# Turning the recurrence's input with a transposing DMA in two f16 halves instead of two TensorE transposes

## What is computed

```
h = rmsnorm(x, norm_g);  proj = h @ w_in            # 4096 x 3072
sb_q, sb_k, sb_v, sb_gate, lru_x, lru_gate, xa_q, xa_gate = split(proj)
sb_out  = stick_breaking_attention(rmsnorm(q), rmsnorm(k), v)     # 8 heads x 64
xc      = causal_depthwise_conv(lru_x, conv_w, conv_b)            # width 4, 256 channels
r, i    = sigmoid(xc @ w_rg + b_rg), sigmoid(xc @ w_ig + b_ig)    # 4 blocks of 64
log_a   = -8 * r * softplus(-lambda)
h_t     = exp(log_a) * h_(t-1) + sqrt(1 - exp(2 log_a)) * (i * xc)   # over time
xa_out  = memory_cross_attention(xa_q, mem)                       # 4 heads, 256 tokens
y       = concat(sb_out * silu(sb_gate), h * silu(lru_gate), xa_out * silu(xa_gate))
out     = x + y @ w_out
```

## Time and profile before

| what | value |
|---|---|
| median of 3 runs | 1570.18 us (1567.96 to 1570.65) |
| the profiled execution | 1568.22 us |
| its span in the trace | 1566.5 us, mean granted TensorE clock 0.994 |
| PE busy | 1514.1 us, 97% of the span |
| DVE busy | 1029.6 us, 66% |
| ACT busy | 882.3 us, 56% |
| POOL busy | 314.7 us, 20% |
| DMA queue q1 (SP's) | 201 MB, 52.8% of 16 engines' time |

### The profile page before, as it was taken

How to read it: one execution, slowest core, us unless ns; L and a number is a source line. 1 busy time by engine, 2 the same in 40 slices (tenths; PEclk the granted TensorE clock), 3 DMA queues, 4 the chain that set the end, 5 groups by cost and what they waited for, 6 DMA issues and landing times.

```text
span 1566.5 us, 29731 instructions
## 1 busy us (share of the span) xinstructions
PE 1514.1 (97%) x10828; PEld 741.4 (47%) x10828; DVE 1029.6 (66%) x1874; ACT 882.3 (56%) x1593; POOL 314.7 (20%) x305
## 2 busy tenths in 40 slices
PE   4899899999999999999999999999999999999996
PEld 1344444444444444444444444444444444444452
DVE  5889566766666666656676666666665667666674
ACT  5887455654455664455565446566445556544661
POOL 2122112222122222111222211222211222221120
PEclk9999999999999999999999999999999999999999
DMA  9355555456455445554545545544556454555545
GB/s 367 136 168 105 132 112 118 111 125 141 117 125 123 104 118 133 125 136 105 123 104 130 141 117 119 129 102 117 136 119 142 104 117 111 127 142 120 120 90 136
DMA packets 425928, 201.63 MB, mean 129 GB/s; under 512 B 394592, under 2 KB 395040, under 8 KB 424736
## 3 DMA queue, kind: packets, MB, share of 16 engines
q1 hardware_dynamic: 425600, 200.98, 52.8%
q10 hardware_dynamic: 288, 0.13, 0.0%
HBM read 55.53 MB, written 50.53 MB: 68 GB/s over the span
## 4 chain that ended last, share of the span: by engine, by line
PE 87%; ACT 4%; DVE 4%; SPq 2%; issue 2%; DMA 1%; POOL 0%; ACTq 0%; DVEq 0%; POOLq 0%
PE bank L1792 26%; PE bank L1793 26%; PE bank L1794 26%; PE bank L1871 2%; SPq L492 2%; PE bank L1986 2%; PE bank L1836 2%; PE bank L1857 1%; PE bank L1880 1%; ACT w_pair L867 1%; PE bank L1926 0%; PE bank L1921 0%; PE bank L1823 0%; PE bank L1923 0%; PE bank L1922 0%
## 5 line engine op out<-in xcount | busy, mean ns | idle before, releaser
L1792 PE MATMUL bank<-w_pair,x_hi 128*128 128x512 f16 x1536 | 585.0, 381 | 13.8 <-DVE w_pair L1231 4.8
L1793 PE MATMUL bank<-w_pair,x_hi 128*128 128x512 f16 x1536 | 584.1, 380 | 0.0
L1794 PE MATMUL bank<-w_pair,x_lo 128*128 128x512 f16 x1536 | 584.0, 380 | 0.0
L1124 ACT ACTIVATE spare<-xy,columns 128x1024 f16<-128x1024 f32 x32 | 36.7, 1148 | 399.6 <-DVE columns L1650 399.6
L1792 PEld LDWEIGHTS bank<-w_pair,x_hi 128*128 128x128 f16 x1536 | 150.7, 98 | 190.1 <-issue 13.9
L1794 PEld LDWEIGHTS bank<-w_pair,x_lo 128*128 128x128 f16 x1536 | 150.7, 98 | 182.6 <-issue 2.4
L1793 PEld LDWEIGHTS bank<-w_pair,x_hi 128*128 128x128 f16 x1536 | 150.8, 98 | 166.4 <-issue 2.5
L1792 PE MATMUL bank<-wo_pair,y_hi 128*128 128x512 f16 x480 | 181.9, 379 | 1.2 <-issue 1.2
L1793 PE MATMUL bank<-wo_pair,y_hi 128*128 128x512 f16 x480 | 181.9, 379 | 0.0
L1794 PE MATMUL bank<-wo_pair,y_lo 128*128 128x512 f16 x480 | 181.9, 379 | 0.0
L736 POOL TENSOR_TENSOR fail_and_take<-fail_and_take,seen 128x512 f32<-128x512 f32 x32 | 42.5, 1327 | 684.2 <-ACT fail_and_take L888 684.2
(11 more groups left out here) (267 smaller groups left out, 2397.8 us busy)
## 6 DMA issues: line engine op xcount, KB each, us to landing
xy<-in_x SPq DMA_DIRECT2D x32, 512.0 KB, 3.6
spare<-in_x SPq DMA_DIRECT2D x31, 512.0 KB, 4.2
out<-spare SPq DMA_DIRECT2D x30, 512.0 KB, 2.7
gate_kept<-gate SPq DMA_DIRECT2D x32, 256.0 KB, 2.3
v_kept<-v_sb SPq DMA_DIRECT2D x32, 256.0 KB, 2.1
fail_and_take<-v_sb SPq DMA_DIRECT2D x64, 128.0 KB, 2.3
q_kept<-q_t SPq DMA_DIRECT2D x32, 256.0 KB, 4.0
k_kept<-k_t SPq DMA_DIRECT2D x32, 256.0 KB, 4.5
```

The lines of the kernel that those rows point to most:

```text
L1124: act.activation(y_halves[:, 0, :], xy[:, :], ACT.Copy, scale=y_top[:, :]).then_inc(s["y_high"], 1)
L1792: pe.matmul(dst, hi[:, k, :], pair[:, 0, k, :], start=k == 0, stop=False)
L1793: pe.matmul(dst, hi[:, k, :], pair[:, 1, k, :], start=False, stop=False)
L1794: last = pe.matmul(dst, lo[:, k, :], pair[:, 0, k, :], start=False, stop=k == KD - 1)
```

## The change

lru_x leaves PSUM as two f16 halves (`lx_halves`): ACT writes the high one in place of the f32 copy, scaled by a power of two (VDOWN); DVE makes the low one in a new instruction in `silu_lru`, 128 x 256 from PSUM, ahead of the instruction that was there. A new transposing DMA of both halves at once (128 x 512 f16) into `lx_turned` is issued by SP ahead of `q_t`'s high half, behind a wait for `gate_l` of the same tile (in step 31: ahead of the low halves). The two transposes on PE go, with their waits. DVE's `convolution` waits for that DMA and adds the two halves into `conv_in` instead of copying from PSUM. The scale that ACT applied is multiplied into the taps once, in step 0. `gate_products` takes over the wait for `y_mixed` that stood ahead of the transposes.

```
--- before.py
+++ after.py
@@ -123,7 +123,7 @@
         q_raw = sb("q_raw", [P, HS, HD])
         k_raw = sb("k_raw", [P, HS, HD])
         xq_raw = sb("xq_raw", [P, HX, HD])
-        lx_raw = sb("lx_raw", [P, LW])
+        lx_halves = sb("lx_halves", [P, 2, LW], F16)
         v_sb = sb("v_sb", [P, 2, 2, GC], F16)
         k_t = sb("k_t", [P, 2, 2, HS // 2, HALF + P], F16)
         q_t = sb("q_t", [P, 2, HS // 2, P], F16)
@@ -146,6 +146,7 @@
         y_halves = spare[:, D:2 * D].bitcast(F16).rearrange("p (a c) -> p a c", a=2)
         xq_halves = spare[:, 2 * D:2 * D + LW].bitcast(F16).rearrange("p (a c) -> p a c", a=2)
         rs_diag = spare[:, 2 * D + LW:2 * D + LW + P]
+        lx_turned = spare[:, 2 * D + LW + P:2 * D + 2 * LW + P].bitcast(F16).rearrange("p (a h t) -> p a h t", a=2, t=P)
         x_halves = x_t32[:, :, :].rearrange("p k t -> p (k t)").bitcast(F16).rearrange("p (a c) -> p a c", a=2)
         h_sb = spare[:, KD * GC - D - LW:KD * GC - D].rearrange("p (h t) -> p h t", t=P)
         ident = sb("ident", [P, P])
@@ -157,6 +158,7 @@
         g_in = given[:, 0:KD]
         g_mem = given[:, KD:2 * KD]
         at = 2 * KD + LH * TAPS
+        taps = given[:, 2 * KD:at]
         cw = given[:, 2 * KD:at].rearrange("p (h j) -> p h j", j=TAPS)
         cb, brg, big, lam = [given[:, at + i * LH:at + (i + 1) * LH] for i in range(4)]
         gq, gk, gxq, gxk = [given[:, at + 4 * LH + i:at + 4 * LH + i + 1] for i in range(4)]
@@ -243,7 +245,7 @@
         HEADS = bank[7]
 
 
-        names = """turned_lx lx_evac k_gained qk_high qk_low k_halo out0_read scores sig masked scan w w_high w_low heads
+        names = """lx_evac k_gained qk_high qk_low k_halo out0_read scores sig masked scan w w_high w_low heads
             q_read k_read xa_read lru_read sg_read v_hi v_read q_sum k_sum xq_sum rs_mid rs_done normed
             gate_x gate_l gate_sb xa_scores mx_done neg_done p_done p_high p_low
             conv gates_done gates_read tanh_done beta_steps ui_done beta_done u_done h_done
@@ -258,6 +260,7 @@
         w_turned = sem("w_turned")
         p_turned = sem("p_turned")
         y_turned = sem("y_turned")
+        lx_arrived = sem("lx_arrived")
         late_y_high = sem("late_y_high")
         x_loaded = sem("x_loaded")
         xt_loaded = sem("xt_loaded")
@@ -591,6 +594,12 @@
                     have_dma(sp, kept["q"], n - 1)
                     have(sp, s["xa_scores"], n - 1)
                     for part, signal in ((0, s["qk_high"]), (1, s["qk_low"])):
+                        if part == (1 if last else 0):
+                            have(sp, s["gate_l"], n)
+                            have(sp, s["lx_evac"], n - 1)
+                            if isinstance(n, int) and n == 0:
+                                sp.wait_ge(m_kv, MT)
+                            turn(lx_turned.rearrange("p a h t -> p (a h) t"), lx_halves[:, :, :].rearrange("p a c -> p (a c)"), lx_arrived)
                         have(sp, signal, n)
                         q_half, k_half, xq_half = halves_of_heads(n, part)
                         turn(q_t[:, part], q_half, qk_turned)
@@ -1059,7 +1068,8 @@
                 if A:
                     have(act, proj_done[3], n)
                     u = unscale[:, G_LRU:G_LRU + 1]
-                    act.activation(lx_raw[:, :], PROJ[1][:, 0:LW], ACT.Copy, scale=u)
+                    have_dma(act, lx_arrived, n - 1)
+                    act.activation(lx_halves[:, 0, :], PROJ[1][:, 0:LW], ACT.Copy, scale=VDOWN)
                     act.activation(gate[:, p, D // 2:D // 2 + LW], PROJ[1][:, LW:GC], ACT.Sigmoid, scale=u
                                    ).then_inc(s["lru_read"], 1)
 
@@ -1360,11 +1370,11 @@
 
                 def convolution(d):
 
-                    have(dve, s["turned_lx"], n - d)
+                    have_dma(dve, lx_arrived, n - d)
                     dve.tensor_copy(conv_in[:, :, 0:TAPS - 1], conv_in[:, :, P:P + TAPS - 1]).then_inc(s["halo"], 1)
                     have(dve, s["halo"], n - d)
-                    dve.tensor_copy(conv_in[:, :, TAPS - 1:], SMALL[:, 2 * P:4 * P].rearrange("p (h t) -> p h t", t=P)
-                                    ).then_inc(s["lx_evac"], 1)
+                    dve.tensor_tensor(conv_in[:, :, TAPS - 1:], lx_turned[:, 0, :, :], lx_turned[:, 1, :, :], ALU.add
+                                      ).then_inc(s["lx_evac"], 1)
                     have(dve, s["lx_evac"], n - d)
                     if isinstance(n, int) and n == 1:
                         dve.wait_ge(qk_turned, 96)
@@ -1480,6 +1490,9 @@
                     weights_low(1)
 
                 def silu_lru():
+                    have(dve, s["lru_read"], n)
+                    dve.scalar_tensor_tensor(lx_halves[:, 1, :], PROJ[1][:, 0:LW], VDOWN, lx_halves[:, 0, :],
+                                             ALU.mult, ALU.subtract)
                     silu(s["lru_read"], s["gate_l"], PROJ[1][:, LW:GC], slice(D // 2, D // 2 + LW), G_LRU)
 
                 def silu_stick():
@@ -1508,6 +1521,7 @@
                 if first:
                     next_chunk(4)
                     chunk_factor(5)
+                    w_next(dve.tensor_scalar(taps, taps, unscale[:, G_LRU:G_LRU + 1], 1.0 / VDOWN, ALU.mult, ALU.mult))
                     silu_lru()
                     chunk_low(5)
                     silu_stick()
@@ -1815,13 +1829,6 @@
 
                 def near_scores(d):
 
-                    have(pe, s["lru_read"], n - d)
-                    have(pe, s["y_mixed"], n - 2)
-                    if d == 0:
-                        have(pe, s["gates_read"], n - 1)
-                    for c in range(LH):
-                        last = pe.transpose(SMALL[:, (2 + c) * P:(3 + c) * P], lx_raw[:, c * P:(c + 1) * P], ident[:, :])
-                    last.then_inc(s["turned_lx"], 1)
                     if static and n == 1:
                         pe.wait_ge(zeroed, 5)
                     have(pe, qk_turned, n - d, 96)
@@ -1861,6 +1868,7 @@
                 def gate_products(d):
 
                     have(pe, s["conv"], n - d, TAPS)
+                    have(pe, s["y_mixed"], n - 2)
                     if d == 0:
                         have(pe, s["sig"], n)
                     if static and n == 1:
@@ -1909,8 +1917,6 @@
                         pe.wait_ge(mv_made, 2)
                     if X and spreads(n + 1):
                         have(pe, s["x_scaled"], n + 1)
-                    if last_one:
-                        have(pe, s["lx_evac"], n)
                     if after:
                         have(pe, s["y_mixed"], n - 2)
                     hi_t, lo_t = probs_of(n - 1)[1:]
```

More of the change, by code:

```diff
@@ L1816, in near_scores @@
                 def near_scores(d):
[L1818 to L1824, removed]
                     if static and n == 1:
```

## The result

The changed kernel takes 1576.45 us (median of 5 runs, 1575.76 to 1576.63). The kernel before, with two further runs on the same chip, takes 1569.43 (5 runs, 1567.96 to 1570.65). The ratio is 1.0046 with a 95% interval of 1.0035 to 1.0056: 7.0 us slower. The forecast was 1575.0 and slower. The profiled execution took 1576.52 us with a span of 1574.8; before had 1568.22 and 1566.5.

What follows compares the result with a forecast made beforehand. PE was taken to bound the loop, SP's chain 0.57 us a step shorter. 1.35 + 0.36 + 0.69 + 3.1 - 0.42 = +5.1 us on 1570.18 gives 1575.3, rounded to 1575; range 1564 to 1582.

Steps and rivals of the forecast that it cites:

- PE's saving, 0.21 a tile: On PE between product and scores: dropping the two transposes saves 0.53 - 0.32 = 0.21 us a tile, at most 0.31.
- SP's delay, 0.90: In SP's queue: the new turn ahead of q_t makes everything behind it 0.90 us later, bounds 0.77 to 1.12.
- Where SP's chain starts: Second chain beside PE's: from PE's third product over ACT and DVE to qk_high, SP, x_lo, PE; 0.57 us a step shorter.
- The room, 0.57: Between x_lo's issue on SP and PE's use of it: x_lo could come 0.55 to 0.60 us later before PE waits.
- The step, +0.12: Each loop step: 0.90 - 0.57 - 0.21 = +0.12 us, bounds -0.11 to +0.34; 26 steps give +3.1.
- The form of the wait: PE's waits in the profile after: a row for x_lo with about 28 entries of 0.33 us each.
- Steps 0 to 3, +1.35: Start of the run: 0.1 us in step 0 and 0.4 in step 1 on DVE, 0.85 in step 2 on SP.
- Step 4, +0.36: Start of x_lo's product on PE in step 4: room only 0.33 us, so 0.90 - 0.33 - 0.21 = +0.36.
- Step 5, +0.69: Start of x_lo's product on PE in step 5: no room, so 0.90 - 0.21 = +0.69 us.
- The end, -0.42: Step 31: no rows are turned, so the transposes of tiles 30 and 31 come off in full, -0.42 us.
- Hidden: Rival: SP's delay is 0.57 us or less, PE keeps its saving; about -5.5 us, 1564.7 us; chance 0.13.
- The whole turn is late: Rival: gate_l comes after qk_high, delay 1.37 us on SP, 0.59 a step; +18.8 us, 1589 us; chance 0.1.

Runs made afterwards that it cites:

- e1: The changed kernel without the new turn; the convolution adds the two halves unturned, so values are not the layer's: 1562.75 us.
- e2: The changed kernel, complete, with the new turn and its waits moved behind the turns of x_hi and x_lo on SP (last step unchanged): 1565.49 us.
- e3: The changed kernel with two f32 transposes of the identity put back at the old place on PE, result unused: 1581.42 us.
- e6: The changed kernel, complete, with SP's new turn waiting for the low half itself, not the gate's product behind it on DVE: 1567.84 us.
- e4: The changed kernel with a second turn, of the high half alone (128 x 256 f16), right behind the new one: 1614.9 us.
- e5: The changed kernel with the new turn taking only the high half (128 x 256), which the convolution adds to itself: 1576.17 us.

## Why the prediction came out right

The direction and the cause were right. That the time was only 1.45 us off is in part luck: the median of 3 runs that it was counted from lies 0.75 above the median of 5. As a difference it is 5.1 forecast against 7.0 measured. Step by step:

*PE's saving, 0.21 a tile.* 46.35 - 46.13 = 0.22 in e1 and e2, and 0.18 in e3 the other way round. Right.

*SP's delay, 0.90.* Against the memory's scores `q_t` is later by 633.76 - 619.83 - 13.08 = 0.85 in the one kind of step and by 0.74 in the other; `x_lo` by 1.04 and 0.72, on average 0.88. So 0.90 is right on average for `x_lo`, but not by its own working: `q_t` is 0.80 later, since the new turn and its gap took 1.30, not 1.35, and in the other kind of step the turn starts 0.57 ahead of the old place of `q_t`, not 0.45; the queue then adds 0.08 behind `q_t`. In the one kind of step the new turn starts 632.46 - 619.83 = 12.63 behind the memory's scores, as forecast (627.75 - 615.12).

*Where SP's chain starts.* The prediction had it run from PE's third product over ACT and DVE to `qk_high`. In the changed kernel it leaves PE behind the second product, crosses POOL for 4.59 us and reaches SP over `gate_l`. The sum doesn't hang on this: it needs only that the scores lie ahead of the product where the chain starts, which is so of both.

*The room, 0.57.* On average it is that: over 24 steps of before PE starts 3.71 behind the issue of `x_lo`. By the kind of step it is 0.54 and 0.60. e6 and the change bracket it: delays of 0.61 and 0.35 cost 0.03 a step, 0.88 costs, and a turn more costs a turn.

*The step, +0.12.* This is the term that was mis-sized: it is +0.16 on the average of the steps from 6 to 30, which is 24 x 0.16 = 3.9 instead of 2.9. With what the profile shows the sum would have been 0.88 for the delay, and 0.06 because PE starts on average 3.24 and 3.16 after the issue of `x_lo` in the two kinds of step (mean 3.20) and not 3.14, less 0.57 and less 0.22: 0.15. The prediction took the 3.14 of a single step of before for a constant. The first and the last of the 26 steps cost more: the one up to the start of step 6 +0.38, the one up to the start of step 31 +0.69, with a wait of 0.72.

*The form of the wait.* Forecast were about 28 entries of 0.33 in each step alike; there are 13 entries of 0.44 (5.7 / 13) between 300 and 1400 us, in every other step, and between them stalls of 0.15 that the view does not list. By the distances of the starts, as above, PE stands on average for 0.60 and 0.14 in the two kinds of step; the mean, 0.37, is near the forecast; whoever takes the missing entries as proof that the steps alternate between waiting and not waiting reads too much into the view. The landing of `x_lo` stayed at 3.1 in the median, so this sign of being wrong did not show.

*Steps 0 to 3, +1.35.* 181.43 - 179.12 = 2.31 (before's value from its trace), less the 1.02 of chance: 1.29. *Step 4, +0.36:* 229.81 - 227.14 = 2.67, so +0.36. *Step 5, +0.69:* 277.58 - 273.93 = 3.65, so +0.98, again with the longer wait in such a step. *The end, -0.42:* with step 31 at 1487.54 against 1478.94 the change is 8.6 behind, and 8.3 at the end, so -0.3.

*The sum.* 1.29 + 0.36 + 0.98 + 4.95 (steps 6 to 31) - 0.3 = 7.3, forecast 5.1; of the 2.2 between them 1.85 are in the steps 6 to 31.

*The rivals.* "Hidden" needs a delay below 0.57, and e6 shows it at 0.45. "The whole turn is late" is what e4 does with the second one: 1.2 to 1.3 a step. Neither was the case of the change, whose turn starts 0.45 or 0.57 ahead of the old place of `q_t`; 0.45 was forecast.

*Left open.* Why the steps alternate. In every other step SP takes 1.47 from the start of `x_hi` to that of `x_lo`, in the others 1.33, and in the same steps PE starts 3.24 instead of 3.16 after `x_lo`'s issue (averages over the loop). In two successive steps `x_lo` starts 12.82 to 12.85 after `q_t` in before, e1 and e2; in the change it is 13.01 and 12.82, in e6 12.98 and 12.83, and 13.00 in a step of e3. This extra comes in the kernels where the new turn lies ahead of `q_t` on SP. The bytes don't bring it: with half of them, in e5, it is 13.01 and 12.82 again. Another 0.18 is there before SP's queue: the new turn starts 12.63 behind the memory's scores in the one kind of step and 12.44 in the other, and DVE's first product with POOL's `rs` 7.13 and 6.95. e2, where PE never waits in the loop, has such a difference at `q_t` too (12.99 and 12.80). What brings either about, and why in every other step, no run tells.

## What to carry to other kernels

A queue that issues one transfer behind the other is an engine: before something is put on it, measure how much later than now the last transfer on it may start, and what of the new work falls into its idle time. Here 1.3 us of issue met some 0.5 of idle time and 0.57 of room. The 0.2 or so left over, with some 0.15 by which the queue and the landing grew, took PE's 0.22 and put 0.16 on top, while the page's line of busy time does not list SP at all. The same transfer behind the urgent ones, or released 0.4 us sooner by its own signal, turned a loss of 7 us into a gain of 4 and into a draw: place first, then cost.

## What was not expected of the hardware

A DMA that transposes 128 x 256 f16 held SP's queue for 1.17 us, one of 128 x 512 for 1.19 and the rows' of 128 x 1024 for 1.23 to 1.28: a quarter of the data saves less than a tenth. And size isn't all: `xq_t`, 128 x 256 too, takes 1.25. From issue to landing it was 2.3, 2.4 and 3.1 us in the median.

Steps that all do the same work alternated between 46.6 to 46.8 and 46.3 us; 0.19 of the difference arises in SP's own queue, 0.14 of it between the turns of `x_hi` and `x_lo`.

Two f32 transposes of 128 x 128 in a stream of matmuls cost 0.22 us, while the trace gives the pair a length of 0.38.
